# One weight split at the end of a stage, moved from VectorE to GpSimd

## The reference

```python
# first network, 2 layers
hm = rms_norm(h, g_mlp[l])
h = h + jnp.square(jax.nn.relu(hm @ w_mlp_in[l])) @ w_mlp_out[l]
gate = jax.nn.sigmoid(rms_norm(h, g_ple[l]) @ w_ple_gate[l])
h = h + gate * (p[l] @ w_ple_proj[l])
...
# second network, 4 layers
h = h + 0.5 * swiglu(rms_norm_2(h, norm_ffn1[i]), ffn1_w_gate_up[i], ffn1_w_down[i])
hn = rms_norm_2(h, norm_mix[i])
...
h = h + mix
h = h + 0.5 * swiglu(rms_norm_2(h, norm_ffn2[i]), ffn2_w_gate_up[i], ffn2_w_down[i])
```

## Time and profile before

| | |
|---|---|
| median of 3 runs | 2742.37 us |
| profiled execution, its own time | 2742.88 us |
| its span (first to last instruction) | 2741.1 us |
| mean granted TensorE clock | 0.983 of full speed |
| busy share: TensorE matmul, VectorE, ScalarE, GpSimd | 96%, 64%, 49%, 1% |

### The profile page before, as it was taken

One profiled execution on the slowest core, in us unless ns is written; L12 is line 12 of the kernel. 1 busy time (PEld: TensorE's weight loads), 2 busy tenths in 40 slices (PEclk: granted clock), 3 DMA queues, 4 the chain that ended last, 5 costly groups with the idle time before them and its releaser, 6 DMA issues.

```text
span 2741.1 us, 38304 instructions
## 1 busy us (share of the span) xinstructions
PE 2641.4 (96%) x14934; PEld 2261.0 (82%) x14934; DVE 1742.7 (64%) x1911; ACT 1342.6 (49%) x1551; POOL 16.4 (1%) x19
## 2 busy tenths in 40 slices
PE   7899998999899999999999999999999999999998
PEld 7688886888788888888888788888878888888887
DVE  7666576655766657666666666666656666665665
ACT  5444454444644545455444544544655454454543
POOL 0000000000000000000000000000000000000000
PEclk9799997999999999999999999999999999999999
DMA  7155451554455435555543355455225545543451
GB/s 286 57 178 192 160 192 62 179 193 169 158 202 192 154 108 184 186 179 189 192 160 129 147 185 195 173 192 190 108 94 193 195 172 192 189 155 123 169 192 69
DMA packets 63398, 454.61 MB, mean 166 GB/s; under 512 B 7088, under 2 KB 7344, under 8 KB 8768
## 3 DMA queue, kind: packets, MB, share of 16 engines
q1 hardware_dynamic: 61920, 448.82, 45.1%
q0 software_dynamic: 944, 3.18, 0.3%
q10 hardware_dynamic: 432, 1.14, 0.1%
HBM read 452.06 MB, written 1.05 MB: 165 GB/s over the span
## 4 chain that ended last, share of the span: by engine, by line
PE 87%; DVE 5%; ACT 4%; issue 2%; DMA 1%; SPq 0%; DVEq 0%; ACTq 0%
PE tb L473 23%; PE tb L471 13%; PE acc L258 9%; PE acc L260 9%; PE acc L259 9%; PE tb L470 3%; PE acc L227 2%; ACT w_hi L200 2%; DVE w_lo L207 2%; PE acc L229 2%; PE acc L230 2%; PE tb L289 1%; PE acc L799 1%; PE acc L801 1%; PE acc L800 1%
## 5 line engine op out<-in xcount | busy, mean ns | idle before, releaser
L207 DVE TENSOR_TENSOR w_lo<-raw,w_hi 128x2048 fp32r<-128x2048 f32 x426 | 976.4, 2294 | 368.2 <-ACT w_hi L200 367.4
L200 ACT ACTIVATE w_hi<-raw 128x2048 fp32r<-128x2048 f32 x426 | 814.1, 1912 | 368.5 <-PE acc L260 301.7
L473 PE MATMUL tb<-xT,w_hi 128*128 128x512 f32 x2772 | 987.8, 396 | 0.0
L471 PE MATMUL tb<-xT,w_lo 128*128 128x256 f32 x3168 | 818.5, 279 | 0.0
L471 PEld LDWEIGHTS tb<-xT,w_lo 128*128 128x128 f32 x3168 | 597.0, 188 | 33.8
L473 PEld LDWEIGHTS tb<-xT,w_hi 128*128 128x128 f32 x2772 | 520.2, 188 | 107.1
L258 PE MATMUL acc<-w_hi,cat 128*128 128x512 f32 x1024 | 403.1, 394 | 6.7 <-issue 3.5
L259 PE MATMUL acc<-w_hi,cat 128*128 128x512 f32 x1024 | 399.7, 390 | 0.0
L260 PE MATMUL acc<-w_lo,cat 128*128 128x512 f32 x1024 | 399.6, 390 | 0.0
L258 PEld LDWEIGHTS acc<-w_hi,cat 128*128 128x128 f32 x1024 | 193.0, 188 | 46.9 <-issue 4.2
L260 PEld LDWEIGHTS acc<-w_lo,cat 128*128 128x128 f32 x1024 | 192.9, 188 | 41.0
(11 more groups left out here) (336 smaller groups left out, 3229.8 us busy)
## 6 DMA issues: line engine op xcount, KB each, us to landing
raw<-in_stream SPq DMA_DIRECT2D x426, 1024.0 KB, 4.8
h<-in_x SPq DMA_DIRECT2D x2, 512.0 KB, 4.9
gain<-in_gains POOLq DMA_DIRECT2D x2, 512.0 KB, 9.1
xn<-in_gates POOLq DMA_DIRECT2D x2, 512.0 KB, 8.7
out<-xn SPq DMA_DIRECT2D x2, 512.0 KB, 2.7
cst<-in_consts ACTq DMA_DIRECT2D x1, 960.5 KB, 12.1
big<-in_pT POOLq DMA_DIRECT2D x2, 256.0 KB, 3.0
big<-in_lam_qk POOLq DMA_DIRECT2D x1, 256.0 KB, 11.4
```

The costliest lines, as they stand in the source:

```text
L200: act.activation(w_hi[:, k % SPLIT, :], raw[:, k % RAW, :], ACT.Copy).then_inc(hi_done, 1)
L207: dve.tensor_tensor(w_lo[:, k % SPLIT, :], raw[:, k % RAW, :], w_hi[:, k % SPLIT, :], ALU.subtract).then_inc(lo_done, 1)
L471: last = pe.matmul(banks[f][:, 0:SEQ], lo, xT[:, kt, 0, :], start=False, stop=False)
L473: last = pe.matmul(banks[f], hi, both, start=False, stop=kt == KT - 1)
```

## The change

The low split of chunk c+1 at the end of each `mlp` and of each `ffn` but the last (2 + 7 = 9 places) is taken out of VectorE's program and done by GpSimd, by the new function `pool_lo`. GpSimd waits until the high split of c+1 is done and until the low split of c is counted. VectorE's low split of c+2 now first waits for `lo_done` to show that c+1 is done. To leave the split out in the last turn alone, VectorE's last turn of every `ffn` is now written out behind the loop (before: only in the last `ffn`).

```diff
+        def pool_lo(pool, k):
+
+            pool.wait_ge(hi_done, k + 1)
+            pool.wait_ge(lo_done, k)
+            pool.tensor_tensor(w_lo[:, k % SPLIT, :], raw[:, k % RAW, :], w_hi[:, k % SPLIT, :],
+                               ALU.subtract).then_inc(lo_done, 1)
...
                     hidden_lo(j + 1, i)
-                    split_lo(dve, c, 4 + 3 * j + SPLIT, i)
-
-            repeat(dve, (PAIRS_B - 1) // 2, f == 2 * DEPTH_B - 1, turn)
+                    if j == 0 or not (isinstance(i, int) and i == LAST_TURN):
+                        split_lo(dve, c, 4 + 3 * j + SPLIT, i)
+
+            LAST_TURN = (PAIRS_B - 1) // 2 - 1
+            repeat(dve, LAST_TURN + 1, True, turn)
             residual(dve, n, c + CHUNKS_FFN - 1, row_scale)
...
+                if kind == "mlp":
+                    pool_lo(pool, c + CHUNKS_MLP - 2 + SPLIT)
+                if kind == "ffn" and l != 2 * DEPTH_B - 1:
+                    pool_lo(pool, c + CHUNKS_FFN - 2 + SPLIT)
                 if kind == "ple":
                     pool.wait_ge(*when("h_new", (n - 1, 1, 1)))
                     pool.dma_start(p_in, pT[l, :, :, :]).then_inc(*sig("p_in", l, 16))
...
-                    if last_kind != "ffn":
+                    if last_kind not in ("ffn", "mlp"):
                         split_lo(dve, c, -2 + SPLIT)
+                    elif kind != "end":
+                        dve.wait_ge(lo_done, c - 1 + SPLIT)
                     if kind != "mlp":
                         split_lo(dve, c, -1 + SPLIT)
```

## The result

The changed kernel takes 2723.23 us, the median of 4 runs (2719.07 to 2725.73), against 2742.6 us for the kernel before beside it. The ratio is 0.9926, 95% interval 0.9906 to 0.9946: 0.74% faster, where 2725.4 us and 0.62% were predicted. A second comparison, later and with its own runs of the kernel before (median 2744.34 us), gave 2722.7 us (5 runs, 2714.83 to 2725.07), ratio 0.9915, interval 0.9901 to 0.9929. The profiled execution's span fell from 2741.1 to 2723.9 us, by 17.2.

What follows compares the result with a forecast made beforehand. TensorE, busy 96%, was taken as the bound, so only its waits counted: 2742.88 - 10.1 (`ffn` ends) - 6.9 (`ple` starts) = 2725.9, less 0.5 for the runs' median, 2725.4 us (0.62% faster); range 2722 to 2733.

Steps and rivals of the forecast that it cites:

- What bounds, and where: TensorE, busy 96%, bounds; it waits for c+1's split at seven `ffn` ends (9.0 us) and two `ple` starts (6.6 us).
- The `ffn` ends, 7 x 1.44: TensorE's transposes wait for residual adds behind VectorE's low split; removing it saves 1.44 us at each of seven, 10.1 us.
- The control: At the `mlp` end no split precedes the residual; transposes come 0.24 us after the matmul, so the whole 1.44 should go.
- The `ple` starts, 2 x 3.46: TensorE's second chunk waits for VectorE's late low split; 3.46 us saved at each of two, 6.9 us.
- wait for c+2 or c+3: In `ple`, later splits should not replace the removed wait: c+2 ready 1.2 us early, c+3 with 1.6 us left.
- GpSimd's 4.75 us and the room of 10.3: Each GpSimd subtraction takes 4.75 us, with 10.3 us of room at an `ffn` end, 10.7 in `ple`; costs nothing.
- the fourth rival: GpSimd's split is late, delaying VectorE's c+2 split, scale factor and TensorE; at 14 us the time is 2758; chance 0.03.
- `p_in`: The load for `ple`, moved behind GpSimd's split, is issued about 332.3 and lands about 335 to 338; costs nothing.
- Contention: VectorE's adds and `xT` beside GpSimd's splits, with one operand in PSUM, keep their usual durations; taken as nothing.
- the rival: First rival: every VectorE instruction beside GpSimd is stretched by 1.70, giving 2731.9 us; chance 0.08.
- the upper bound of 8.1 us: Longest GpSimd subtraction assumed: 4.75 x 1.70, the stretch of a VectorE split beside a GpSimd copy; still costs nothing.
- The sum: 2742.88 us for the profiled execution less 10.1 and 6.9 gives 2725.9; median of runs 2725.4, 0.62% faster.

Runs made afterwards that it cites:

- the runs with two and three subtractions: Changed kernel with GpSimd doing each of the nine subtractions twice or three times before counting it: 2723.32 us and 2751.41 us.
- the kernel with three: Changed kernel with GpSimd doing each subtraction three times before counting it: 2751.41 us, ratio 1.0034 to the kernel before.
- the two tried above: Changed kernel plus one VectorE instruction among the residual adds, a two-input SBUF product or a one-input scaling: single executions 2739.18 and 2743.76 us.

## Why the prediction was right

**What bounds, and where.** Right. The two rows of waits named the nine places, both are gone after, and each half restored alone brings its own row back.

**The `ffn` ends, 7 x 1.44.** Right: 1.51 us a stage, 10.6 in all. The control, the `mlp` end of the earlier trace rows, gave the right pattern: the adds after are spaced as there, and the transposes come without a wait.

**The `ple` starts, 2 x 3.46.** Right: 3.60 us in the first. The second shows 2.7, with a granted clock of 0.95 over 675 to 709 us in the changed kernel, where the wait itself is gone as well; at a full clock it is 3.6. No wait for c+2 or c+3 came up.

**GpSimd's 4.75 us and the room of 10.3.** 4.60, and the runs with two and three subtractions put the limit between 9.2 and 13.8 us. The 10.3 us at an `ffn` end is the room until VectorE wants to split c+2, but TensorE can be kept waiting only later. In the kernel with three, GpSimd works from 898.62 to 912.55 and TensorE waits 2.23 us to its end, so its room there is 11.7 us; in `ple`, worked out the same way, it is 10.6, where 10.7 was taken. What TensorE waits for is c+1 itself, and not, as the fourth rival has it, the scale factor behind VectorE's split. So that rival's price was too high: it put 14 us of GpSimd's work 16 us above the kernel before, with TensorE 3.7 us later at an `ffn` end than in the changed kernel; three subtractions came out 9 above, with waits of 2.2 to 2.3. The price that I set for the experiment was too low, 23.7 for 28.2, about what the drops of the clock behind three of the nine waits cost.

**`p_in`.** Issued at 331.45, landed at about 336.9; 335 to 338 were predicted. No wait.

**Contention.** The value taken, nothing, was right: the VectorE rows that overlap the nine splits are 29 adds of 0.74 to 0.75 us and 18 `xT` rows of 0.47 to 0.49, each with one operand in PSUM, and none is longer than elsewhere. The picture behind the rival and behind the upper bound of 8.1 us was wrong. A factor of 1.70 was read from the split that took 3.90 us in the earlier trace rows; but that split began at 1937.56, 0.13 us behind the first of the two copies that the earlier trace rows has in one row:

```profile
1937.43 1.88 POOL L1974 COPY big<-big 32x2048 f32<-32x2048 f32 x1 [1217.44 <-DVE big L1577]
...
1939.26 3.96 POOL L1974 COPY big<-big 32x2048 f32<-32x2048 f32 x1
```

The first copy ends at 1939.31 and the split at 1941.46: 1.75 us of standing and 2.15 of work. Such a rival is not priced by stretching the rows but by the time to GpSimd's end, up to 4.6 us each, and only for instructions like the two tried above. Here there was none, in nine places.

**The sum.** 2725.9 for an execution of 2742.88 became 2725.73 in the profiled run. That this is within 0.2 us is luck: at equal clocks the nine places give 10.6 + 7.2 = 17.8 us where 17.0 were predicted, and between these two executions the clock alone moved `mla` by +2.6, `moba` by -1.5, the first `mix_a` by -0.7, the first `ffn` by -0.9 and the second `ple` by +0.9. The median came 2.2 us lower than predicted, inside the scatter of the runs.

## What to carry to other kernels

A split or copy that runs in front of a chain that the bounding engine waits for costs up to its own duration there (1.5 of 2.29 us here), however idle its engine is elsewhere, and one that stands too late in its engine's order costs its lateness (3.5 us in `ple`): look at what the engine that is waited for did just before. Moving the work within its own engine's order can give nearly as much as moving it to another engine, and has no second engine to contend with; here the runs can't tell the two apart, and the stages put the second engine 1.8 us ahead. If GpSimd takes the work, its slowness matters only beyond the room there is (4.6 of 11.7 us here), and one has to ask which VectorE instructions fall beside it: the adds and `xT` rows with an operand in PSUM ran on, a product or a scaling from SBUF stood until GpSimd was done.

## What the runs showed of the hardware

Some VectorE instructions stood until a GpSimd instruction was done; the adds and `xT` rows with an operand in PSUM did not. A VectorE product of two SBUF inputs, 0.41 us alone, lasted 3.22 beside GpSimd's subtraction and ended 0.28 us behind it, and a scaling with a single SBUF input (0.28 alone) lasted 3.08 and ended 0.16 behind. It goes the other way too: the second GpSimd copy above lasted 3.96 us instead of 1.88, beside 2.15 us of VectorE's split. The Trainium skill says so in "SBUF — State Buffer", section "SBUF: two separate sides": the shared pair of ports is an exclusive lock, held for an instruction, taken by VectorE instructions with two SBUF inputs or in a 2-port mode. The trace agrees for the product. It agrees for the scaling too, if that ran in a 2-port mode, which no run here shows.

A wait of 2.3 us of TensorE cost 4.05 and 4.07 us in two `ffn` stages, since the granted clock then was 0.85 over 11 us, and 2.55 in a third, where it stayed at the full level. Of two waits of 3.31 us in `ple`, in the same execution, one was followed by the lower level and one was not; before the change neither was. What decides this, these runs don't show.
